# Attention's keys in chunks of six over seven banks, the first expert's gather ahead of three weight blocks, and idle products on TensorE at the heads of four stages

## What is computed

```python
def trunk_layer(x, cvec, lw, latent, ctx_k, ctx_v, s0_f, s0_b):
    mod = silu(cvec) @ w_mod + b_mod           # shift1, scale1, gate1, shift2, scale2, gate2
    h = rmsnorm(x, norm1_w) * (1 + scale1) + shift1
    mix = mixer(h)                             # 8 query heads on 2 key heads, plus 4 retention heads
    x = x + gate1 * mix
    h = rmsnorm(x, norm2_w) * (1 + scale2) + shift2
    return x + gate2 * expert_choice_ffn(h)    # 16 experts, each takes its 2 T / 16 best tokens
```

## Time and profile before

| | |
|---|---|
| median of three runs | 3340.36 us (3339.26 to 3342.31) |
| the profiled execution | 3340.56 us |
| its span, first to last instruction | 3338.8 us |
| mean granted TensorE clock | 0.955 |
| PE, DVE, ACT, POOL busy | 93%, 56%, 52%, 12% |
| read from and written to HBM | 319.54 MB, 74.06 MB |

### The profile page before, as it was taken

The page is one execution under the profiler, slowest core; times in us unless marked ns, Lnnn a source line. Parts: engine busy times, 40 slices in busy tenths (PEclk is TensorE's granted clock), DMA queues, the critical chain, the costliest instruction groups (busy, mean ns, idle before and its releaser), DMA issues. The chain is left out here.

```text
span 3338.8 us, 59092 instructions
## 1 busy us (share of the span) xinstructions
PE 3094.8 (93%) x21488; PEld 2812.6 (84%) x21488; DVE 1855.0 (56%) x3219; ACT 1720.8 (52%) x3397; POOL 413.0 (12%) x392
## 2 busy tenths in 40 slices
PE   8999996689999999999799847999999999999995
PEld 5788885578888888888688647999999999999995
DVE  3222227578888888888533384554544545455555
ACT  3222224567777777777433335555454454544454
POOL 0333335300000000000000010111111111111103
PEclk9999998789999999999799858999999999999998
DMA  6221115320000000000164206666565665666656
GB/s 233 79 71 64 64 61 185 114 70 20 28 16 25 22 23 24 19 28 16 46 204 152 88 12 208 190 189 186 182 190 183 185 190 182 189 183 191 189 169 260
DMA packets 316107, 394.60 MB, mean 118 GB/s; under 512 B 30356, under 2 KB 272232, under 8 KB 315000
## 3 DMA queue, kind: packets, MB, share of 16 engines
q1 hardware_dynamic: 305080, 356.11, 32.2%
q0 software_dynamic: 10560, 36.77, 4.9%
q10 hardware_dynamic: 384, 0.62, 0.1%
HBM read 319.54 MB, written 74.06 MB: 118 GB/s over the span
## 5 line engine op out<-in xcount | busy, mean ns | idle before, releaser
L2529 DVE TENSOR_TENSOR e_w_lo<-e_raw,e_w_hi 128x2048 fp32r<-128x2048 f32 x192 | 440.2, 2293 | 489.0 <-ACT e_w_hi L2459 489.0
L93 PE MATMUL e_ps<-e_x_hi,e_w_hi 128*128 128x272 f32 x2048 | 603.0, 294 | 5.5 <-issue 5.5
L95 PE MATMUL e_ps<-e_x_hi,e_w_lo 128*128 128x272 f32 x2048 | 594.7, 290 | 0.0
L94 PE MATMUL e_ps<-e_x_lo,e_w_hi 128*128 128x272 f32 x2048 | 591.1, 289 | 0.0
L1536 DVE TENSOR_TENSOR a_pT_lo<-a_ps_t,a_pT_hi 128x512 fp32r<-128x512 f32 (+1 forms) x648 | 368.5, 602 | 139.2 <-ACT a_pT_hi L1434 138.8
L1434 ACT ACTIVATE a_pT_hi<-a_ps_t 128x512 fp32r<-128x512 f32 (+1 forms) x648 | 319.4, 532 | 173.7 <-PE a_ps_t L1299 168.9
L93 PEld LDWEIGHTS e_ps<-e_x_hi,e_w_hi 128*128 128x128 f32 x2048 | 387.4, 189 | 7.1 <-issue 5.5
L94 PEld LDWEIGHTS e_ps<-e_x_lo,e_w_hi 128*128 128x128 f32 x2048 | 388.2, 190 | 0.0
L95 PEld LDWEIGHTS e_ps<-e_x_hi,e_w_lo 128*128 128x128 f32 x2048 | 386.9, 189 | 0.0
L2459 ACT ACTIVATE e_w_hi<-e_raw 128x2048 fp32r<-128x2048 f32 x192 | 366.1, 1907 | 15.7 <-DMA e_raw<-in_w_gate 11.4
L1509 DVE TENSOR_REDUCE a_mx<-a_ps_s 128x1 f32<-128x896 f32 (+2 forms) x392 | 346.7, 892 | 27.3 <-PE a_ps_s L1289 27.2
(11 more groups left out here) (303 smaller groups left out, 5371.8 us busy)
## 6 DMA issues: line engine op xcount, KB each, us to landing
e_raw<-in_w_gate SPq DMA_DIRECT2D x64, 1024.0 KB, 4.9
e_raw<-in_w_up SPq DMA_DIRECT2D x64, 1024.0 KB, 5.0
e_raw<-in_w_down SPq DMA_DIRECT2D x64, 1024.0 KB, 5.0
s_ret<-p_pr SPq DMA_DIRECT2D x17, 768.0 KB, 3.6
p_raw<-in_w_in SPq DMA_DIRECT2D x8, 1152.0 KB, 18.9
o_cT<-s_ct SPq DMA_DIRECT2D x17, 512.0 KB, 5.0
s_x<-o_x SPq DMA_DIRECT2D x17, 512.0 KB, 5.0
s_xn<-o_xn SPq DMA_DIRECT2D x17, 512.0 KB, 3.5
```

The lines of the kernel that those rows point to most:

```text
L93: nc.tensor.matmul(out, w_hi, x_hi, start=first, stop=False)
L94: nc.tensor.matmul(out, w_hi, x_lo, start=False, stop=False)
L95: return nc.tensor.matmul(out, w_lo, x_hi, start=False, stop=last)
L2529: nc.vector.tensor_tensor(w_lo[n % RING][:, :, :], raw[n % RING][:, :, :], w_hi[n % RING][:, :, :].bitcast(F32), ALU.subtract).then_inc(w_ ...
```

## The change

Five edits; which values are computed stays as it was.

1. `busy` issues products of the identity with itself (128 × 128, fp32) into a bank that is overwritten later and that nobody reads: 32 behind the modulation in project, 20 before and 16 behind the turning of the first queries in attention, 28 in the output projection (behind the wait for `wr`), 32 before and 16 behind the first expert's turning.
2. Attention's head: the queries come first. Keys are loaded, split and subtracted six tiles at a time (`k_all`, `k_hi`, `k_lo` hold all 18 tiles, in SBUF that the probabilities' buffers take over), and turned into seven banks: the two of ps_t and the five of ps_s. ACT evicts 11 tiles, DVE the other 7 (i mod 5 is 1 or 3).
3. Values are loaded in one DMA, and POOL makes their halves, in four operations, once DVE has made the last k_lo. PE waits for them before the first product with them, ACT before the first eviction into `pT_hi`.
4. Experts' head: SP issues block 0, then waits for the gather, then issues the others. Only block 0 is split ahead of the rows; ACT evicts even column groups and DVE odd ones.
5. x_hi and x_lo of expert 0 are made in two halves, and PE starts on the first; blocks 1 and 2 are split behind them.

```diff
@@ project, PE
             turn_modulation(NG - 1)
+            busy(nc, g, psP[0][:, 0:P], 32)
             over_tiles(pe, body)

+def busy(nc, g, out, count):
+
+    for _ in range(count):
+        nc.tensor.matmul(out, g["ident"][:, :], g["ident"][:, :], start=True, stop=True)

@@ attention
+        CHUNK = 6
+        NCH = NK // CHUNK
+        BY_DVE = (1, 3)
 ...
+        with ExitStack() as early:
+            k1 = Core(nc, early)
+            k_hi, k_lo = (k1.sb(f"a_k_{n}", [P, NK, NKV, 2, HD], F32R) for n in ("hi", "lo"))
+            k_all, v_all = (k1.sb(f"a_{n}_all", [P, NK, KV_W]) for n in ("k", "v"))
+        pT_hi, pT_lo = [], []
+        for i in range(2):
+            pT_hi.append(k.sb(f"a_pT_hi{i}", [P, KEY_TILES, GROUP, P], F32R))
+            pT_lo.append(k.sb(f"a_pT_lo{i}", [P, KEY_TILES, GROUP, P], F32R))
 ...
+        key_banks = [p[:, :, :] for p in ps_t] + [ps_s[:, b, :].rearrange("p (c t) -> p c t", c=4) for b in range(5)]
+
+        def keeper(i):
+
+            return int(i % 5 in BY_DVE)
+
+        def keeps(i):
+
+            return sum(keeper(n) == keeper(i) for n in range(i + 1))
+
+        def spread_heads(rows):
+
+            return rows.rearrange("p a (v o f) -> p (a v) o f", v=NKV, o=1).broadcast_to([P, CHUNK * NKV, 2, HD])
+
 ...
@@ attention, SP
-            def load_kv(h, off):
-                if not known(h, off, 0) and not known(h, off, 1):
-                    sp.wait_ge(vals_ok, 4 * h + 2 * off - 2)
-                sp.dma_start(kv_row[off % 2][:, :], pick(s["kv"], h, off)).then_inc(kv_in[off % 2], 16)
-
-            over_pairs(sp, load_kv, 2, NTA // 2, 0)
             sp.dma_start(q_row[:, :, :].rearrange("p h f -> p (h f)"), s["q"][0]).then_inc(q_in, 16)
+            for n in range(NCH):
+                at = slice(CHUNK * n, CHUNK * (n + 1))
+                sp.dma_start(k_all[:, at, :], s["kv"][at, :, 0:KV_W].rearrange("a p n -> p a n")).then_inc(kv_in[n], 16)
+            sp.dma_start(v_all[:, :, :], s["kv"][:, :, KV_W:].rearrange("a p n -> p a n")).then_inc(v_in, 16)
@@ attention, POOL
+            pool.wait_ge(v_in, 16)
+            pool.wait_ge(k_lo_ok, NCH)
+            src = v_all[:, :, :].rearrange("p a (v f) -> p a v f", v=NKV)
+            for v in range(NKV):
+                nc.gpsimd.tensor_copy(vals[:, :, v, 0, :], src[:, :, v, :]).then_inc(vals_ok, 1)
+            for v in range(NKV):
+                pool.wait_ge(vals_ok, v + 1)
+                nc.gpsimd.tensor_tensor(vals[:, :, v, 1, :], src[:, :, v, :], vals[:, :, v, 0, :].bitcast(F32), ALU.subtract)\
+                    .then_inc(vals_ok, 1)
@@ attention, PE
+            def turn_keys(i):
+                pe.wait_ge(k_hi_ok, i // CHUNK + 1)
+                pe.wait_ge(k_lo_ok, i // CHUNK + 1)
+                if i < 2:
+                    pe.wait_ge(emptied[i], 1)
+                if i >= len(key_banks):
+                    pe.wait_ge(k_kept[keeper(i - len(key_banks))], keeps(i - len(key_banks)))
+                for n, part in enumerate((k_hi, k_lo)):
                     for v in range(NKV):
-                        ins = nc.tensor.transpose(ps_t[j][:, 2 * n + v, :],
-                                                  part[:, v, :, :].bitcast(F32).rearrange("p d f -> p (d f)"),
-                                                  g["ident"][:, :])
-                ins.then_inc(k_turned, 1)
-
-            over_pairs(pe, key_tile, 2, NTA // 2, 0)
-            pe.wait_ge(k_kept, NK)
-            pe.wait_ge(vals_ok, 2 * NK)
-            pe.wait_ge(fold_ok, 3)
+                        ins = nc.tensor.transpose(key_banks[i % len(key_banks)][:, 2 * n + v, :],
+                                                  part[:, i, v, :, :].bitcast(F32).rearrange("p d f -> p (d f)"), g["ident"][:, :])
+                ins.then_inc(k_turned[keeper(i)], 1)
 ...
+                    if isinstance(t, int) and t == 0 and grp == 0:
+                        pe.wait_ge(vals_ok, 2 * NKV)
 ...
             start = Bank(-1)
+            busy(nc, g, ps_o[:, 0, :], 20)
             for half_at in range(2):
                 turn_queries(0, half_at, start)
+            busy(nc, g, ps_o[:, 0, :], 16)
+            for i in range(NK):
+                turn_keys(i)
+            for who in range(2):
+                pe.wait_ge(k_kept[who], sum(keeper(i) == who for i in range(NK)))
+            pe.wait_ge(fold_ok, 3)
@@ attention, ACT
+            def keys_hi(n):
+                at = slice(CHUNK * n, CHUNK * (n + 1))
+                act.wait_ge(kv_in[n], 16)
+                nc.scalar.activation(k_hi[:, at, :, :, :].rearrange("p a v o f -> p (a v) o f"),
+                                     spread_heads(k_all[:, at, :]), ACT.Copy).then_inc(k_hi_ok, 1)
+
+            def keep_keys(i):
+                act.wait_ge(k_turned[0], keeps(i))
+                nc.scalar.activation(keys[:, :, :, i * P:(i + 1) * P].rearrange("p n v t -> p (n v) t"),
+                                     key_banks[i % len(key_banks)], ACT.Copy).then_inc(k_kept[0], 1)
 ...
+                    if isinstance(i, int) and i == 0 and n == 0:
+                        act.wait_ge(vals_ok, 2 * NKV)
                     nc.scalar.activation(out, ps_t[b][:, 0:out.shape[1], :], ACT.Copy).then_inc(hi_kept, 1)
 ...
             queries_hi(0)
+            keys_hi(0)
             start = Bank(-1)
             for half_at in range(2):
                 leave(0, 0, "q", half_at, *start.next())
+            for n in range(1, NCH):
+                keys_hi(n)
+            for i in range(NK):
+                if keeper(i) == 0:
+                    keep_keys(i)
@@ attention, DVE
+            def keys_lo(n):
+                at = slice(CHUNK * n, CHUNK * (n + 1))
+                dve.wait_ge(k_hi_ok, n + 1)
+                nc.vector.tensor_tensor(k_lo[:, at, :, :, :].rearrange("p a v o f -> p (a v) o f"), spread_heads(k_all[:, at, :]),
+                                        k_hi[:, at, :, :, :].bitcast(F32).rearrange("p a v o f -> p (a v) o f"), ALU.subtract)\
+                    .then_inc(k_lo_ok, 1)
+
+            def keep_keys(i):
+                dve.wait_ge(k_turned[1], keeps(i))
+                nc.vector.tensor_copy(keys[:, :, :, i * P:(i + 1) * P].rearrange("p n v t -> p (n v) t"),
+                                      key_banks[i % len(key_banks)]).then_inc(k_kept[1], 1)
 ...
             queries_lo(0)
+            for n in range(NCH):
+                keys_lo(n)
+            for i in range(NK):
+                if keeper(i) == 1:
+                    keep_keys(i)
@@ output_projection, PE
+            busy(nc, g, ps_w[1][:, 0, 0:P], 28)
             mix(0, 0, 0)
@@ experts, SP
             for n in range(PER):
+                if n == 1:
+                    sp.wait_ge(xg_in, 48)
                 if n >= RING:
                     sp.wait_ge(w_lo_ok, n - RING + 1)
@@ experts, PE
                 if c == 0:
                     pe.wait_ge(xg_in, (e + 1) * 48)
-                if c >= 2:
+                if isinstance(e, int) and e == 0:
+                    if c >= 2:
+                        pe.wait_ge((xT_ok, xT_odd)[b], c // 2 * 2)
+                elif c >= 2:
                     pe.wait_ge(xT_ok, e * 2 * DC + (c - 1) * 2)
 ...
+                        if isinstance(e, int) and e == 0 and q == 0 and c == DC // 2:
+                            pe.wait_ge(x_hi_ok, 1)
+                            pe.wait_ge(x_lo_ok, 1)
 ...
             def body(e, last):
-                pe.wait_ge(x_hi_ok, e + 1)
-                pe.wait_ge(x_lo_ok, e + 1)
+                if isinstance(e, int) and e == 0:
+                    pe.wait_ge(x_hi_half, 1)
+                    pe.wait_ge(x_lo_half, 1)
+                else:
+                    pe.wait_ge(x_hi_ok, e + 1)
+                    pe.wait_ge(x_lo_ok, e + 1)
 ...
+            busy(nc, g, ps[0][:, 0:P], 32)
             for c in range(DC):
                 turn_rows(0, c)
+            busy(nc, g, ps[0][:, 0:P], 16)
             over_experts(pe, body)
@@ experts, ACT
-            for n in range(AHEAD):
+            split(0, 0)
+            for c in range(0, DC, 2):
+                rows(0, c)
+            act.wait_ge(xT_ok, 2 * DC)
+            nc.scalar.activation(x_hi[:, 0:DC // 2, :], xT[:, 0:DC // 2, :], ACT.Copy).then_inc(x_hi_half, 1)
+            nc.scalar.activation(x_hi[:, DC // 2:, :], xT[:, DC // 2:, :], ACT.Copy).then_inc(x_hi_ok, 1)
+            for n in range(1, AHEAD):
                 split(0, n)
-            for c in range(DC):
-                rows(0, c)
-            rows_hi(0)
@@ experts, DVE
+            split(0, 0)
+            for c in range(1, DC, 2):
+                dve.wait_ge(x_turned, c + 1)
+                for lo, hi, who in ((0, CAP, LAT), (CAP, SLOTS, CTX)):
+                    nc.vector.tensor_scalar(xT[:, c, lo:hi], ps_t[1][:, lo:hi], g["gain"][:, 1, c, who:who + 1],
+                                            g["mod"][:, SHIFT2 + c, who:who + 1], ALU.mult, ALU.add).then_inc(xT_odd, 1)
```

(18 more changed lines are left out.)

45 lines of the change are left out of this document (3 added, 42 removed).

## The result

| | before | after |
|---|---|---|
| median of 4 runs, us | 3340.66 (3339.26 to 3342.31) | 3313.40 (3312.42 to 3315.52) |
| profiled execution, us | 3340.56 | 3312.42 |
| its span, us | 3338.8 | 3310.7 |
| mean granted clock | 0.955 | 0.967 |

The ratio is 0.9919, with a 95% interval of 0.9907 to 0.9931: 27.3 us faster. The forecast was 38.1 us faster (3302.3), and the range went to 3314.0, so the result lies 0.6 us inside its slow edge.

What follows compares the result with a forecast made beforehand. PE, or the PE-ACT-DVE ring, bounds each stage, so gains lie at stage heads where PE waits. 22.8 + 2.7 + 0.2 − 1.8 + 12.9 + 1.4 − 0.1 = 38.1 us off 3340.36 gives 3302.3, range 3293 to 3314.

Steps and rivals of the forecast that it cites:

- its own case: Whole kernel: the summed forecast, 3302.3 us, holds within 3297 to 3307; chance 0.63.
- Rival 1: Stage heads: idle products don't carry the clock over the waits behind them; about 3310 us, chance 0.18.
- signs named beforehand: Trace marks at the stage heads that would show the forecast right, such as first scores about 18 us after attention's first issue.
- Keys, 22.8 forecast: Attention's head: first scores after 17.9 us instead of 40.6, 22.8 us won.
- V on POOL: Attention: POOL makes V's halves in 8.6 us (5.7 to 11.3), done at 653 to 657, cost 0.
- rivals 2 and 4: Attention: 2, V late, 3304 to 3313 us, chance 0.09; 4, POOL's strided passes far dearer, slower than before, chance 0.02.
- Clock behind the keys, 2.7 forecast: Attention's first scores: high clock instead of low wins 2.7 us, between 0 and 3.5.
- Project, 0.2 forecast: Project stage: faster first matmuls, but PE then meets DVE; 0.2 us won, between −0.3 and 2.5.
- Output, −1.8 forecast: Output projection's head: 28 idle products behind the router-weights wait lose 1.8 us net, between −2.5 and 0.
- Experts' head, 12.9 forecast: First expert: gather lands 4.2 us after issue, first product at 2015.3; 12.9 us won, between 9 and 15.
- Clock at the experts, 1.4 forecast: First expert's first products: higher clock wins 1.4 us, between 0 and 2.6.
- SP's new wait: First expert: weight blocks 1 to 3 queue behind the gather; cover 2 us, cost 0.

Runs made afterwards that it cites:

- experiment 1: The kernel after with half the idle products in each of its six runs of them; 3308.68 us.
- experiment 5: The kernel before with the keys' part of the change alone and no idle products; 3315.98 us, ratio 0.9920.
- experiments 2: The kernel after without any idle product; 3307.40 us.
- experiment 8: The kernel after with idle products refitted: none in project, 10 and 8 at keys, 14 in output ahead of the router-weights wait, 30 and 8 at experts; 3303.35 us.
- 4: The kernel before with the experts' part of the change alone and no idle products; 3331.75 us, ratio 0.9971.

## Why the prediction was right, and where its terms were off

The direction, the order of the heads and the main term were right; the forecast was 11.1 us too fast (of the gain, 10.0 are missing in the spans and 10.8 in the medians). The measured time is inside the stated range by 0.6 us, outside the 3297 to 3307 that the prediction gave its own case, and no rival describes what happened: that the range held it is in part luck. The bounds named with the terms don't give the 3296 and 3314 either; added up they make gains of 48.5 and 24.8 us, so 3292 to 3316. Rival 1 was not the reason for the shortfall at the keys; what the clock did at the experts is told below.

Of the signs named beforehand, the first scores came 19.1 us after attention's first load (18 named), at the high clock, and the first pT_hi was released by PE. The first expert product came 21.3 us after the first load of its weights (16 named), the first product of the output stage 7.0 us later, reckoned from the issue of the router weights (4 to 5 named), and tile 1's transposes in project waited for nothing, where DVE had been named.

- **Keys, 22.8 forecast, 21.5 measured.** The step "PE: 20 idle products ... I take 0.213 and 0.107 each" failed. The price came from transposes and was put on products, each of which took two records, 0.213 us apart at the low clock and 0.112 at the high one: 0.427 and 0.22 us. The second run therefore ended 2.4 us behind k_lo(0), not "hardly behind" it. With half as many products (experiment 1, which is what the sum in effect had priced) the head is 18.1 us, where the forecast had 17.9 from the first load, 18.2 as the table measures.
- **V on POOL: right.** Copies 1.12 us each, subtractions 2.63, in all 7.5 us where I took 8.6 and bounded at 5.7 and 11.3. The "GPSIMD Engine Reference" of the Trainium skill (its section on reconciling with measured numbers) gave 1.0 us a copy, and with it 7.6 in all, as an estimate: this case's trace agrees, with 1.1 and 7.5. V was issued at 635.60 and landed 9.5 us later, at 645.1, just as DVE made the last k_lo (645.11); that is between the 643 of the price by bytes and the 648 of the price by pieces, with w_out's loads beside it. The slower rivals 2 and 4 did not come true. By the page "DMA: Bandwidth & Descriptors" of the Trainium skill (Specifications) 512 bytes is still a line-rate size; a landing midway, beside other loads, neither shows that nor speaks against it.
- **Clock behind the keys, 2.7 forecast, 2.6 measured** (first scores to the second head's exp 10.3 us, 12.9 before; the whole of attention behind the first scores shows 1.9, within its scatter). The amount was right: the fall in the wait for the first exp, for which 3.5 had been cut to 2.7, came. In experiment 5, where the clock stays high there, the ten products take 2.63 us and the second exp comes 9.4 us behind the first scores, the full 3.5 less than before. The cause was wrong: the gap-free transposes do it, as experiments 2 and 5 show.
- **Project, 0.2 forecast.** The stretch up to attention was 0.4 us longer, within its scatter of 4 us; over all kernels it averages 633.6 us with idle products in the project stage (five kernels) and 633.4 without (six). The 32 products took 7.4 us and the first real one came 1.6 us later than before, at the high clock. The structure was right: PE then meets DVE. PE of the kernel after:

```profile
68.07 0.47 PE L93 MATMUL p_psP<-p_w_hi,p_hhi 128*128 128x512 f32 x1 [0.97 <-DVE p_w_lo L422]
...
97.56 1.97 PE L259 MATMUL p_psT<-ident,p_x 128*128 128x128 f32 x8 [3.02 <-DVE p_x L407]
```

And of the kernel before:

```profile
97.45 1.11 PE L259 MATMUL p_psT<-ident,p_x 128*128 128x128 f32 x8 [2.99 <-DVE p_x L406]
```

The faster products end in a wait for DVE at 68.07 that the kernel before doesn't have, and at 97.5 both kernels stand at the same wait, 0.1 us apart.
- **Output, −1.8 forecast, −4.6 measured.** Same failed step: "28 products at the low clock are 6.0 us" were 8.25 us, even with the clock's rise midway (4.8 forecast for that case). The structure (behind the wait for the router weights, nothing to absorb it) was right. What I didn't ask is what the products would do ahead of that wait, where PE idled for 11 us: 14 of them there make the head 2.3 us shorter than before instead of 4.6 longer (1.1 to 2.6 against all the kernels without idle products there).
- **Experts' head, 12.9 forecast, 7.75 measured**, from three terms. The gather took 5.5 us to release PE, not 4.2 (+1.3; from 4.5 to 5.9 over the kernels with the wait, so the lower bound served as the estimate). xT was whole 7.05 us after the landing, not 5.7 (+1.35): "four rows 1.0 to 1.1 apart" are pairs 1.5 us apart at the high clock and 1.8 at the low one, because on each bank the transposes and the eviction (0.82) alternate. And PE came 2.6 us late out of its 16 idle products: the same doubled price, at the low clock (at the high one 16 of them would be about 3.6 us instead of 6, an estimate from the keys' second run, and PE nearly on time). Together 5.3 us, where 5.15 are missing.
- **Clock at the experts, 1.4 forecast, 2.0 measured** between the two traces, 1.8 over all kernels. It was not carried over the turning, where the clock fell, as rival 1 has it; the second run raised it again before the first real product.
- **SP's new wait**: PE never waited for a block of the first expert's weights, so cost 0, as forecast; its worth, which I had not priced apart, is 1.6 to 2.9 us of the head.

All in all, the doubled price accounts for 2.6 us at the experts, 2.8 at the output stage and about 1.3 at the keys, 6.7 of the 10 missing; the experts' gather and rows account for 2.7. The rest, 0.6 us, lies in stretches with a larger scatter. The split is an account from single traces, good to about 1 us a head. The doubling could have been read before: the gate products of the output stage, eight calls, are counted x16 at L1752 above, and the kernel before has the same row, x16 and 1.95 us, at its line 1715.

## What to carry to other kernels

Before pricing an instruction by "the same shape" in a trace, compare the count of records with the count of calls: here an fp32 product shows two records where an fp32 transpose shows one. Products that only keep the clock up belong ahead of the wait that PE stands in, fitted to end before it does; behind it each one is on the path (14 ahead: an output head of 18.7 us; 14 behind: 22.1). Where real work comes dense they bring little: the keys' head is 17.8 to 18.1 us with 10 and 8 of them, 18.6 to 19.1 without. When a chain starts from a gather, hold the bulk loads back behind it.

## What was not expected of the hardware

The clock fell at about 1994.5 us while PE was busy for 2.60 of the 3.70 us up to 1994.7, in gaps of at most 0.4 us, behind 5.3 us of full work at the high clock (the last window of the experts' head above). In experiment 8 the same part of the turning, with the same gaps, kept the high clock (columns as there):

```profile
1983.50:1987.20 3.70, 2.64 (x15) 1.48 (x13) 2.14 (x6) 2.31 (x6) 0.00 (x0) 1.00 0.96 316
```

The clock held there over gaps of 0.97 and 1.43 us too, and behind the first scores a wait of 3.0 us cost it in the kernel after and not in experiment 5. So none of these gaps decides by itself; what does stays open, and no experiment was made for it. The gather of the first expert's rows, three transfers, released PE between 4.5 and 5.9 us after its last issue in kernels with the same load ahead of it (2 and 4), a spread that no row here explains.
